# One decoder kernel: the first weight block by halves, an operand in one run, bias copies in the first MLP, dilated attention by head pairs, the last tile by halves

## Chip, cores and metric

One Trainium2 chip, one core. The metric is the time of one execution in device microseconds (us), all three transformer parts in one launch. Engines are named as in the profile: PE (TensorE), DVE (VectorE), ACT (ScalarE), POOL (GpSimd), SP (SyncE, which issues every DMA); PEld is PE's weight load.

## What is computed

256 tokens of width 1024 in float32 pass a gated-linear-attention layer with an MLP, a sliding-window-attention layer with an MLP, and a second block with two attentions, two gates, an MLP and a gated extra input:

```python
h = h + gla_mixer(rmsnorm(h), a_w_in, ...)          # 4 heads, chunks of 64
h = h + (relu(rmsnorm(h) @ w_up) ** 2) @ w_down     # MLP 1, 1024 -> 4096 -> 1024
h = h + swa_mixer(rmsnorm(h), ...)                  # 16 heads of 64, window 128, bias by distance
h = h + MLP 2
x = rmsnorm(h, ln_final)
z = rmsnorm(x) @ w_in_2                              # qa ka va | qb kb vb | ga gb
y_a = full attention, 8 heads of 128, axial rope     # "full"
y_b = for 4 head indices h, over 3 dilations g:      # "dilated", 12 heads of 64
      sc = q k^T + bias[g, h];  softmax over all 3 x 256 keys together;  sum p v
x = x + (sigmoid(ga + b) * (y_a @ w_a) + sigmoid(gb + b) * (y_b @ w_b)) @ w_out_2
x = x + MLP 3
x = x + sigmoid(rmsnorm(x) @ w_ple_gate) * (p @ w_ple)
out = rmsnorm(x)
```

## The kernel before

Every large product runs as three products of rounded parts (`prod`, L272): stationary high by moving high, high by low, low by high. A weight block of 2048 columns of 128 partitions (1 MB) passes through rings of three: SP loads it into `raw`, ACT rounds it into `whi` (`highs_to`), DVE subtracts for `wlo` (`lows_to`, two halves). SP issues block j when `wlo` of block j-3 is there. 160-odd blocks follow one another in the order of the products; `weights_to(n)` in `sync_program` (L2295) places the other loads between them by block number. Blocks 0 to 12 are the first layer's input (0, 1: q; 2: a narrow gate; 3, 4: k; 5 to 8: v; 9 to 12: gate), 13 to 16 its output, 17 to 48 MLP 1. All DMAs are issued by SP into one queue.

The activations are transposed on PE (`norm_turn`), evicted by ACT as high part and by DVE as low part into `hT`. In the up projection (`gemm_up`, L318) the weights are stationary and one product takes high and low of `hT` together through `hT2` (512 columns, two runs of 256 that lie 2048 elements apart), a second the high part alone with the low weights (256 columns). The down projection has the activations stationary and 512 weight columns moving.

Every engine runs generators that are interleaved by hand: `run_all((a, 1), (b, 2))` takes one step of a and two of b in turn until both end. In the dilated attention (PE L764, DVE L1464, ACT L2025) the work is by head index h (4) and half of the queries c (2): PE computes the scores of three dilations (64 rows of the array, 3 products), DVE adds the bias and takes the maximum, ACT the exponential with its sum, DVE the shares, PE six transposes, ACT copies them out of PSUM, PE six products with the values (64 columns of the array). It is interleaved with the weight products of gate `ga` (8 steps of 12 products), then the full attention (`full`, L852) with those of gate `gb` (8 steps). Each attention's last heads run after the last step.

The bias by distance is built once: rows of table values go to DRAM (`scr1`, `scr2`), and two DRAM-to-DRAM copies spread them to `toe1` (16 x 128 x 256) and `toe2` (12 x 128 x 384), each row shifted by one. They stand before `weights_to(9)` (L2331 to L2334), and the tables are read into SBUF later (`bias`, L2340 and L2342).

The window attention (`swa`, PE) already works on two heads at a time, in rows 0 to 63 and 64 to 127 of the array for the scores and in columns 0 to 63 and 64 to 127 for the values, one head's products after the other's in the order of the program.

At the end `w_ple_gate` is multiplied in two column halves f and two token halves c; ACT takes the sigmoid, DVE multiplies and adds to x, ACT squares with a sum, POOL makes the root, DVE scales x, SP writes four tiles.

## Time and profile before

| | us |
|---|---|
| median of 3 runs (lowest, highest) | 1064.34 (1063.89, 1066.04) |
| the profiled execution | 1064.24 |
| its span | 1062.4 |
| PE busy | 1012.1 |
| DVE busy | 676.2 |
| ACT busy | 489.3 |
| PE's share of the chain that ended last | 85% |

The span is from the first to the last instruction. A PE product is counted with its drain, so neighbouring products overlap in the records, and a busy PE can still be waiting between them; the distance between starts tells the pace. PEclk is the granted clock as a share of 2.4 GHz. The chain of waits follows the last instruction back, at each step to what released it.

### The profile page before, as it was taken

The page shows a single profiled execution, that of the slowest core. Times are in us where ns is not written, and L with a number is a line of the kernel's source. Part 1 is how long each engine was busy: PE and PEld are TensorE (multiplying, and loading weights), DVE is VectorE, ACT ScalarE, POOL GpSimd, SP SyncE. Part 2 cuts the span into 40 slices and gives each one's busy share as a digit, 9 for nine tenths or more (in the row PEclk, how much of TensorE's full clock was granted, in tenths as well). Part 3 has the DMA queues.
Part 4 walks back from the last instruction along what each step waited for, and adds up shares of the span by engine and source line. Part 5 has one row for each costly group of instructions (what it writes and reads, how often), then busy time and mean ns, then how long its engine had stood idle before and what let it go on. Part 6 is the DMA issues. An engine that isn't in the chain of part 4 may idle for free.

```text
span 1062.4 us, 12980 instructions
## 1 busy us (share of the span) xinstructions
PE 1012.1 (95%) x5384; PEld 849.5 (80%) x5384; DVE 676.2 (64%) x945; ACT 489.3 (46%) x573; POOL 42.8 (4%) x57
## 2 busy tenths in 40 slices
PE   6989999999999889999999999899999999999996
PEld 5866778888888767888888889877877788888875
DVE  4665766566656885754666656676656675466664
ACT  4353445344445653544444454334563454344452
POOL 1000100000000000000000013300000000000000
PEclk9989999999999999999999999999999999999999
DMA  7772376545564314765455555632335656545451
GB/s 214 249 262 80 119 238 224 173 160 197 199 214 143 120 50 149 250 217 197 159 188 180 201 183 161 196 100 80 99 109 178 195 175 215 188 159 197 180 175 43
DMA packets 115027, 180.99 MB, mean 170 GB/s; under 512 B 4351, under 2 KB 78567, under 8 KB 114968
## 3 DMA queue, kind: packets, MB, share of 16 engines
q1 hardware_dynamic: 114968, 180.16, 50.8%
q8 instruction: 42, 0.69, 0.3%
q14 instruction: 17, 0.14, 0.0%
HBM read 179.05 MB, written 5.55 MB: 174 GB/s over the span
## 4 chain that ended last, share of the span: by engine, by line
PE 85%; DVE 7%; ACT 2%; DMA 2%; POOL 2%; issue 1%; SPq 0%; DVEq 0%; POOLq 0%; ACTq 0%
PE ps L265 82%; PE ps L269 3%; DMA raw<-in_a_w_in 2%; DVE wlo L941 2%; DVE M L949 1%; DVE M L941 1%; POOL st L2186 1%; ACT M L1692 1%; ACT RR L1695 1%; ACT whi L1695 1%; POOL M L2186 0%; DVE M L945 0%; ACT M L1695 0%; DMA x<-in_x 0%; POOL st L2183 0%
## 5 line engine op out<-in xcount | busy, mean ns | idle before, releaser
L265 PE MATMUL ps<-whi,RR 128*128 128x512 f32 (+2 forms) x1568 | 494.6, 390 | 9.7 <-DVE wlo L941 6.0
L1695 ACT ACTIVATE whi<-raw 128x2048 fp32r<-128x2048 f32 (+1 forms) x161 | 302.3, 1881 | 196.6 <-PE ps L265 179.9
L941 DVE TENSOR_TENSOR wlo<-raw,whi 128x1024 fp32r<-128x1024 f32 (+1 forms) x322 | 372.5, 1200 | 29.9 <-ACT whi L1695 29.7
L265 PE MATMUL ps<-RR,whi 128*128 128x512 f32 (+1 forms) x1248 | 362.8, 357 | 10.9 <-DVE RR L949 5.6
L265 PEld LDWEIGHTS ps<-whi,RR 128*128 128x128 f32 x1568 | 293.9, 189 | 74.8 <-issue 9.6
L265 PE MATMUL ps<-wlo,RR 128*128 128x512 f32 (+2 forms) x784 | 303.2, 387 | 0.0
L265 PE MATMUL ps<-RR,wlo 128*128 128x256 f32 (+1 forms) x1008 | 284.5, 282 | 0.0
L265 PEld LDWEIGHTS ps<-RR,whi 128*128 128x128 f32 x1248 | 220.3, 190 | 50.6 <-issue 8.3
L265 PEld LDWEIGHTS ps<-RR,wlo 128*128 128x128 f32 (+1 forms) x1008 | 191.5, 190 | 0.9
L265 PEld LDWEIGHTS ps<-wlo,RR 128*128 128x128 f32 x784 | 148.4, 189 | 27.7
L941 DVE TENSOR_TENSOR M<-M,ps 128x512 f32<-128x512 f32 x56 | 38.5, 687 | 181.7 <-ACT M L1695 173.8
L1695 ACT ACTIVATE M<-ps 128x512 f32<-128x512 f32 (+2 forms) x97 | 57.1, 597 | 173.7 <-PE ps L265 138.5
L265 PE MATMUL ps<-M 128*64 128x128 f32 (+5 forms) x416 | 66.4, 334 | 5.6 <-DVE M L949 2.9
L265 PEld LDWEIGHTS ps<-M 128*64 128x64 f32 (+2 forms) x416 | 46.6, 163 | 22.1 <-issue 13.2
L1695 ACT ACTIVATE RR<-M 128x512 fp32r<-128x512 f32 x48 | 30.4, 633 | 71.1 <-DVE M L949 71.1
L2183 POOL TENSOR_SCALAR st<-st 128x2 f32<-128x2 f32 (+3 forms) x13 | 7.7, 595 | 886.6 <-DVE st L1032 621.3
L269 PE MATMUL ps<-ident,M 128*128 128x128 f32 (+1 forms) x194 | 29.4, 290 | 13.3 <-DVE M L941 4.9
L1695 ACT ACTIVATE RR<-ps,G 128x256 fp32r<-128x256 f32 x64 | 25.1, 480 | 32.9 <-PE ps L269 32.8
L269 PEld LDWEIGHTS ps<-ident,M 128*128 128x128 f32 (+1 forms) x194 | 23.2, 148 | 20.9 <-issue 14.9
L949 DVE SCALAR_TENSOR_TENSOR M<-M 128x512 f32<-128x512 f32 (+1 forms) x49 | 34.4, 703 | 1.6
L949 DVE SCALAR_TENSOR_TENSOR RR<-ps,G,RR 128x256 fp32r<-128x256 f32 x64 | 26.4, 478 | 13.7 <-ACT RR L1695 13.7
L941 DVE TENSOR_TENSOR RR<-M,RR 128x512 fp32r<-128x512 f32 x48 | 32.9, 686 | 0.0
(88 smaller groups left out, 381.7 us busy)
## 6 DMA issues: line engine op xcount, KB each, us to landing
raw<-in_w_up SPq DMA_DIRECT2D x32, 1024.0 KB, 5.4
raw<-in_w_down SPq DMA_DIRECT2D x32, 1024.0 KB, 5.0
raw<-in_w_ff SPq DMA_DIRECT2D x32, 1024.0 KB, 5.3
raw<-in_w_in SPq DMA_DIRECT2D x23, 1024.0 KB, 5.1
raw<-in_a_w_in SPq DMA_DIRECT2D x12, 1024.0 KB, 7.1
raw<-in_a_w_out SPq DMA_DIRECT2D x4, 1024.0 KB, 5.0
raw<-in_b_w_q SPq DMA_DIRECT2D x4, 1024.0 KB, 5.3
raw<-in_b_w_out SPq DMA_DIRECT2D x4, 1024.0 KB, 5.0
```

What stands on the lines that cost most here:

```text
L265: return pe.matmul(out, lhsT, rhs, start=start, stop=stop, skip_group_check=True)
L269: return pe.transpose(out, in_, ident[0:n, 0:n])
L941: return dve.tensor_tensor(out, a, b, op)
L949: return dve.scalar_tensor_tensor(out=out, in0=a, scalar=s, in1=b, op0=op0, op1=op1)
L1692: return act.activation(out, in_, f, **k)
L1695: return act.activation(out, in_, ACT.Copy, **k)
L2183: return pool.tensor_scalar(out, a, s1, s2, op0, op1)
L2186: return pool.tensor_tensor(out, a, b, op)
```

## The change

- `hT` and `hT2` share one layout, high and low of a chunk side by side: the 512 columns are one run.
- Block 0 is loaded, rounded and subtracted by halves, ahead of the second half of x, and its products begin with the first four chunks. Nine products of ones (`spin`) stand before the transposes. PE's row scale and the first eviction move behind block 1.
- `toe1` and `toe2` are written in four copies each, behind blocks 19 to 26; the first `bias` load moves from block 21 to 30.
- Dilated attention by pairs of head indices p (2) and halves c: six score products alternate between the rows of the array, twelve value products between its columns; one reduction, two exponentials and two shares. ACT copies the 768 columns in one instruction; its order is in the diff. PSUM banks 3, 4, 5 hold the scores, 6 and 7 the transposes, 2 the outputs. It runs beside ten steps of the gates' products, the full attention beside the remaining six.
- The last column half is cut in tiles `LAST` of 512, 256 and 256; the gain is multiplied in while the root is made, DVE and ACT each scale one token half.

The diff, cut to its core:

```diff
-        self.hT, self.yT = parts(0), parts(4096)
-        self.hT2 = RR[:, 0:4096].rearrange("p (a k t) -> p k a t", a=2, t=T)
+        self.hT2 = RR[:, 0:4096].rearrange("p (k n) -> p k n", k=8)
+        self.hT, self.yT = (self.hT2[:, :, 0:T], self.hT2[:, :, T:2 * T]), parts(4096)
...
-ORDER_D = [(h, c) for h in range(4) for c in range(2)]
+ORDER_D = [(p, c) for p in range(2) for c in range(2)]
+LAST = [(0, 0, 512), (1, 0, 512), (0, 512, 1024), (1, 512, 768), (1, 768, 1024)]
...
-                        for w_ in due(ready(k)):
+                        for w_ in due(K.at("w_lo", (0, 0) if j == 0 and k < 4 else j), ready(k)):
                             pe.wait_ge(*w_)
...
+                        mm(b[:, i, :], hi[:, k, 128 * i:128 * i + 128], V.hT2[:, k, :], k == 0, False)
                         t = mm(b[:, i, T:2 * T], lo[:, k, 128 * i:128 * i + 128], hT[0][:, k, :], False, k == 7)
...
+    def spin(n):
+        for w in due(K.at("ones")):
+            pe.wait_ge(*w)
+        for _ in range(n):
...
     def after_qk(f):
-        if f == 0:
+        if f == 256:
             rows_scale(0)
         count["qk"] += 1
-    g = gemm_a(("qk",), W, 0, 1024, hT, h_ready(0), None, after_qk)
+    g = gemm_a(("qk",), W, 0, 1024, hT, h_ready(0), lambda: None, after_qk)
     for _ in range(4):
         next(g)
...
+            tile = ("ds", p, c)
+            take(tile, 3, 4, 5)
...
-                t = mm(out, V.QB[r0:r0 + 64, hh // 2, c * 128:c * 128 + 128], V.KB[r0:r0 + 64, hh // 2, :], True, True)
+            for j, g in ((0, 2), (0, 0), (1, 1), (0, 1), (1, 2), (1, 0)):
+                if (j, g) == (1, 0):
+                    for w in due(K.at("ds_mid", (p, c))):
+                        pe.wait_ge(*w)
+                r = slice(64 * j, 64 * j + 64)
+                t = mm(b[:, 768 * j + 256 * g:768 * j + 256 * g + 256], V.QB[r, 2 * g + p, c * 128:c * 128 + 128],
+                       V.KB[r, 2 * g + p, :], True, True)
+                if (j, g) == (0, 2):
+                    t.then_inc(*K.up("ds_mid", (p, c)))
...
+            tile = ("dt", p, c, j)
+            take(tile, 6, 7)
...
+                take(tile, 2)
             b = K.bank(tile)
...
+                K.value["di_read", (p, c)] = K.full(tile)
             else:
-                t.then_inc(*K.up("di_read", (h, c)))
+                t.then_inc(*K.up("di_read", (p, c)))
         scores(*ORDER_D[0])
-        for i in range(11):
-            if 0 <= i - 1 < 8:
...
+        for i in range(4):
+            if i:
+                values(*ORDER_D[i - 1])
+            turned(*ORDER_D[i], 0)
+            yield
+            turned(*ORDER_D[i], 1)
+            if i < 2:
+                scores(*ORDER_D[i + 2])
+            yield
+        values(*ORDER_D[3])
     def rope():
...
-    gg = gemm_b(("ga",), W2, 3840, 1024, hT, ready, pairs=0)
+    def gates_b():
+        yield from gemm_b(("ga",), W2, 3840, 1024, hT, ready, (0, 0))
+        yield from gemm_b(("gb",), W2, 4864, 1024, hT, ready, (0, 1))
+    gg = gates_b()
     mix = dilated()
     next(mix)
-    run_all((gg, 1), (mix, 2))
-    gg = gemm_b(("gb",), W2, 4864, 1024, hT, ready)
+    for _ in range(10):
+        next(gg)
+        next(mix, None)
...
+    ready = h_ready(6)
+    for f in (0, 512):
+        bs = acc_pair()
+        tiles = [(("pg", i), take(("pg", i), misc() if i == 4 else bs[LAST[i][0]])) + LAST[i]
+                 for i in range(5) if LAST[i][1] // 512 * 512 == f]
+        for k0 in (0, 4):
+            j, hi, lo = block(A["w_ple_gate_2"][0][k0 * 128:k0 * 128 + 512, f:f + 512], 4, 512)
+            for tile, b, c, n0, n1 in tiles:
...
+                    t = prod(b[:, 0:n1 - n0], hT[0][:, k, c * 128:c * 128 + 128], hT[1][:, k, c * 128:c * 128 + 128],
+                             hi[:, k - k0, n0 - f:n1 - f], lo[:, k - k0, n0 - f:n1 - f], k == 0, k == 7)
...
-    norm_rest(0)
-    lows_to(1)
+    def first_low(i):
+        h = slice(1024 * i, 1024 * i + 1024)
+        for w in due(K.at("w_hi", (0, 0) if i == 0 else 0)):
+            dve.wait_ge(*w)
+        tt(V.lo[:, 0, h], V.raw[:, 0, h], V.hi[:, 0, h].bitcast(F32), ALU.subtract).then_inc(
+            *K.up("w_lo", (0, 0) if i == 0 else 0))
+    norm_early(0)
+    first_low(0)
+    norm_turn(0, 2)
+    norm_turn(0, 3)
+    first_low(1)
+    block["lo"] = 1
     squares(0, *all_x(K, 0))
...
-                V.BB[:, h:h + 5:4, c0:c0 + 256], ALU.mult, ALU.add)
-            stt(s[:, 512:768], b[:, 1, 0:256], rs, V.BB[:, 8 + h, c0:c0 + 256], ALU.mult, ALU.add).then_inc(
+            for w in due(K.full(tile), K.dma("bias", 1), *rb(4), *([K.full(("dt", p - 1, c, 1))] if p else [])):
+                dve.wait_ge(*w)
+            b = K.run(tile, 1536)
+            for j in range(2):
+                h = slice(768 * j, 768 * j + 768)
+                t = stt(s[:, h].rearrange("p (g k) -> p g k", g=3), b[:, h].rearrange("p (g k) -> p g k", g=3),
+                        st[:, 6 + c:7 + c], V.BB[:, 2 * p + j:2 * p + j + 9:4, c0:c0 + 256], ALU.mult, ALU.add)
+            t.then_inc(*K.emptied(tile))
+            for w in due(K.empty(tile)):
+                dve.wait_ge(*w)
+            dve.tensor_reduce(v[:, 0:2], s.rearrange("p (j k) -> p j k", j=2), AX, ALU.max, negate=True).then_inc(
+                *K.up("di_max", (p, c)))
+        def shares(p, c):
+            v = cc(p, c)
+            for j in range(2):
+                s = V.di_s(c)[:, 768 * j:768 * j + 768]
+                for w in due(K.at("di_exp", (p, c, j))):
+                    dve.wait_ge(*w)
+                d = step(dve.reciprocal(v[:, 4 + j:5 + j], v[:, 2 + j:3 + j]))
+                for w in due(d):
+                    dve.wait_ge(*w)
+                ts(s, s, v[:, 4 + j:5 + j], None, ALU.mult, None).then_inc(*K.up("di_p", (p, c, j)))
+        def parts(p):
+            tile = ("do", p)
+            for w in due(K.at("di_hi", p)):
+                dve.wait_ge(*w)
...
+        d = step(tt(s, s, V.PW[:, c, n0:n1], ALU.mult))
+        for w in due(d, K.full(("nt", 6, 3)), x_ready(K, 6, c, n)):
+            dve.wait_ge(*w)
+        tt(xc, xc, s, ALU.add).then_inc(*K.up("x_end", i))
+    def gain(i):
...
+    take()
+    gain(0)
+    gain(1)
+    take()
+    for i in (2, 3, 4):
+        add(i)
+    for i in (2, 3, 4):
+        gain(i)
+    for n in range(2):
+        s = V.SG[:, 1, 512 * n:512 * n + 512]
+        for w in due(K.at("rstd", ("end", 1)), K.at("x_gain", 4)):
+            dve.wait_ge(*w)
+        ts(s, s, st[:, 49:50], None, ALU.mult, None).then_inc(*K.up("y_end", (1, n)))
...
-    norm_rest(0)
-    highs_to(1)
+    def first_high(i):
+        h = slice(1024 * i, 1024 * i + 1024)
+        for w in due(K.dma("w_first") if i == 0 else K.dma("w0", 0)):
+            act.wait_ge(*w)
+        copy(V.hi[:, 0, h], V.raw[:, 0, h]).then_inc(*K.up("w_hi", (0, 0) if i == 0 else 0))
+    norm_early(0)
+    first_high(0)
+    norm_turn(0, 2)
+    norm_turn(0, 3)
+    first_high(1)
+    block["hi"] = 1
     squares(0, *all_x(K, 0))
...
+        soft(*ORDER_D[0])
+        yield
+        yield
+        soft(*ORDER_D[1])
+        yield
+        for i in range(4):
+            turned(i, 0)
+            if 0 < i < 3:
+                soft(*ORDER_D[i + 1])
+            if i == 2:
+                parts(0)
+            yield
+            turned(i, 1)
+            if i < 3:
+                yield
+        parts(1)
...
+    def square(i):
+        c, n0, n1 = LAST[i]
+        for w in due(K.at("x_end", i)):
+            act.wait_ge(*w)
+        actf(V.PW[:, c, n0:n1], x[:, c, n0:n1], ACT.Square, scale=1.0 / 32, accum_out=st[:, 40 + i:41 + i]).then_inc(
+            *K.up("end_sq", i))
...
+        for w in due(K.at("rstd", ("end", 0)), K.at("x_gain", 2)):
+            act.wait_ge(*w)
+        copy(s, s, scale=st[:, 48:49]).then_inc(*K.up("y_first", (0, n)))
...
     xd = A["x"].rearrange("a (c p) d -> p (a c) d", p=128)
     for n in range(2):
         load("x%d" % n, 0, V.x[:, :, n * 512:n * 512 + 512], xd[:, :, n * 512:n * 512 + 512])
+        w = K.blocks[0][0][512 * n:512 * n + 512, :] if K.blocks else A["a_w_in"][0][0:512, 0:256]
+        load("w0" if n else "w_first", 0, V.raw[:, 0, 1024 * n:1024 * n + 1024].rearrange("p (k n) -> p k n", k=4),
+             w.rearrange("(k p) n -> p k n", p=128))
+    state["block"] = 1
     weights_to(4)
     n = 0
...
     weights_to(9)
     for n in range(2):
...
+    for i in range(4):
+        weights_to(19 + i)
+        load("toe1", i, A["toe1"][4 * i:4 * i + 4], bass.AP(tensor=A["scr1"].tensor, offset=127 + 383 * 4 * i, ap=[
+            [383, 4], [-1, 128], [1, 256]]), K.dma("scr1"))
+    for i in range(4):
+        weights_to(23 + i)
+        load("toe2", i, A["toe2"][3 * i:3 * i + 3], bass.AP(tensor=A["scr2"].tensor, offset=127 + 511 * 3 * i, ap=[
+            [511, 3], [-1, 128], [1, 384]]), K.dma("scr2", 2))
+    weights_to(30)
+    load("bias", 0, V.BS, A["toe1"].rearrange("h p c -> p h c"), K.dma("toe1", 3), K.full(("to", 1, 1)))
     weights_to(62)
-    load("bias", 1, V.BB, A["toe2"].rearrange("h p c -> p h c"), K.dma("toe2"), K.empty(("pr", 1, 1)))
+    load("bias", 1, V.BB, A["toe2"].rearrange("h p c -> p h c"), K.dma("toe2", 3), K.empty(("pr", 1, 1)))
     load("lnf", 0, M[:, 0:1024], spread(A["ln_final"]))
     weights_to(109)
...
-    load("bg", 1, V.BG2, spread(A["b_gate_2"][:, 1024:2048]), K.full(("do", 1)))
+    load("bg", 1, V.BG2, spread(A["b_gate_2"][:, 1024:2048]), K.full(("dt", 1, 1, 1)))
     weights_to(117)
     load("p", 0, V.PT, A["p_2"][0, 0].rearrange("(c p) n -> p c n", p=128), K.full(("fv", 7)))
...
-                 V.x[:, c, n * 512:n * 512 + 512], K.at("y_end", (c, n)))
+                 V.SG[:, c, n * 512:n * 512 + 512], K.at("y_end" if c else "y_first", (c, n)))
     for name, n in K.n.items():
         if name.startswith("d_"):
```

## Rows read from the trace of the kernel before

**Rows 1.** Busy time by stretch: stretch, length, engines' busy us, PEclk, DMA share, GB/s
```profile
58.00:66.00 8.00, 3.76 (x17) 2.83 (x16) 3.69 (x4) 4.66 (x4) 0.20 (x1) 0.91 0.80 288
66.00:71.40 5.40, 5.40 (x14) 4.14 (x14) 4.34 (x4) 5.40 (x6) 0.00 (x0) 0.50 0.61 201
130.00:333.00 203.00, 200.76 (x1024) 170.06 (x1022) 125.76 (x143) 93.86 (x86) 1.09 (x3) 1.00 0.59 197
141.00:150.00 9.00, 9.00 (x50) 7.67 (x49) 5.17 (x8) 5.30 (x6) 0.00 (x0) 1.00 1.09 356
```

**Rows 2.** The chain of waits to 80 us: start, us, what
```profile
14.38 17.45 PE ps L265 x122
...
40.08 21.20 DMA raw<-in_a_w_in
...
65.67 8.42 PE ps L265 x24
74.08 0.44 PE ps L269 x4
```

**Rows 3.** Timeline of SP, PE and DVE at the hole: start, us, engine, line, operation
```profile
37.69 2.34 SPq L2293 DMA_DIRECT2D toe<-scr  x2
...
61.04 0.39 PE L265 MATMUL ps<-whi,RR 128*128 128x512 f32 x1
...
55.55 2.43 DVE L1222 TENSOR_TENSOR_SCAN M<-scan,M 128x256 f32<-128x256 f32 x4
```

**Rows 4.** Timeline of ACT at the start
```profile
6.65 3.40 ACT L1695 ACTIVATE RR<-ps,G 128x256 fp32r<-128x256 f32 x8 [1.74 <-PE ps L269]
9.94 1.91 ACT L1695 ACTIVATE whi<-raw 128x2048 fp32r<-128x2048 f32 x1
```

**Rows 5.** Timeline of PE, layer 1 and MLP 1; last row: chain of waits
```profile
23.79 0.28 PE L265 MATMUL ps<-RR,wlo 128*128 128x256 f32 x1
...
24.15 0.28 PE L265 MATMUL ps<-RR,wlo 128*128 128x256 f32 x1
...
205.31 0.39 PE L265 MATMUL ps<-RR,whi 128*128 128x512 f32 x1
205.54 0.28 PE L265 MATMUL ps<-RR,wlo 128*128 128x256 f32 x1
...
216.60 0.40 PE L265 MATMUL ps<-whi,RR 128*128 128x512 f32 x1
216.84 0.40 PE L265 MATMUL ps<-wlo,RR 128*128 128x512 f32 x1
...
1026.68 4.09 PE ps L265 x18
```

**Rows 6.** Timeline of PE in the window attention: scores, then values of a pair
```profile
364.17 0.93 PE L265 MATMUL ps<-M 64*128 64x128 f32 x8
...
365.84 1.14 PE L265 MATMUL ps<-M 128*64 128x128 f32 x12
```

**Rows 7.** Timeline of PE in the dilated attention: a round's parts
```profile
712.30 0.47 PE L265 MATMUL ps<-whi,RR 128*128 128x512 f32 x1
...
715.24 3.01 PE L265 MATMUL ps<-M 64*128 64x256 f32 x18
```

**Rows 8.** Timeline of PE in the full attention: its last rounds and the next projection
```profile
774.29 1.03 PE L265 MATMUL ps<-M 128*128 128x256 f32 x4
...
784.73 0.60 PE L269 MATMUL ps<-ident,M 128*128 128x128 f32 x4
...
788.23 0.47 PE L265 MATMUL ps<-whi,RR 128*128 128x512 f32 x1 [1.02 <-DVE RR L941]
```

**Rows 9.** Timeline of DVE in the dilated attention: the maximum of one head
```profile
706.16 0.95 DVE L1482 TENSOR_REDUCE cc<-M 128x1 f32<-128x768 f32 x1
```

**Rows 10.** Timeline of the end: the last sigmoid and the last scaling
```profile
1053.89 0.67 ACT L1692 ACTIVATE M<-ps,st 128x512 f32<-128x512 f32 x1
...
1058.34 1.41 DVE L949 SCALAR_TENSOR_TENSOR x<-x,st,M 128x512 f32<-128x512 f32 x2 [1.00 <-POOL st L2186]
```

More of the change, by code:

```diff
@@ L91, in pair, with run @@
         return self.banks[:, b:b + 2, 0:n]
+    def run(self, tile, n):
+        b = self.tile[tile][0] if tile in self.tile else 0
+        m = (n + 511) // 512
+        return self.banks[:, b:b + m, :].rearrange("p b n -> p (b n)")[:, 0:n]
     def vacant(self, tile):
@@ L492, in mlp @@
         last_chunk(7)
+    def spin(n):
+        for w in due(K.at("ones")):
+            pe.wait_ge(*w)
+        for _ in range(n):
+            mm(K.banks[:, 3, 0:128], V.S["ones"][:, :], V.S["ones"][:, :], True, True)
+    spin(4)
     tile = ("g", 0)
@@ L764, in dilated, with scores @@
     def dilated():
[L765 to L768 removed]
+        def scores(p, c):
+            tile = ("ds", p, c)
+            take(tile, 3, 4, 5)
+            b = K.run(tile, 1536)
             for w in due(K.empty(("qb", 512)), K.empty(("kb", 512))):
                 pe.wait_ge(*w)
[L771 to L776 removed]
@@ L778, in turned @@
-        def turned(h, c):
-            tile = ("dt", h, c)
-            s = V.di_s(h, c)
-            take(tile, *misc_pair())
-            b = K.pair(tile, 512)
-            for w in due(K.at("di_p", (h, c))):
+            for j, g in ((0, 2), (0, 0), (1, 1), (0, 1), (1, 2), (1, 0)):
[7 more added lines that the diff above has]
+                    t.then_inc(*K.up("ds_mid", (p, c)))
@@ L784, in turned @@
+            t.then_inc(*K.filled(tile))
+        def turned(p, c, j):
+            tile = ("dt", p, c, j)
+            take(tile, 6, 7)
+            b = K.run(tile, 768)
+            for w in due(K.at("di_p", (p, c, j))):
                 pe.wait_ge(*w)
             for n in range(6):
-                out = b[:, 0, n * 128:n * 128 + 128] if n < 4 else b[:, 1, n * 128 - 512:n * 128 - 384]
-                t = tr(out, s[:, n * 128:n * 128 + 128])
+                t = tr(b[:, n * 128:n * 128 + 128], V.di_s(c)[:, 768 * j + n * 128:768 * j + n * 128 + 128])
@@ L788, in turned, with values @@
             t.then_inc(*K.filled(tile))
-        def values(h, c):
-            tile = ("do", h // 2)
-            p = V.di_p(c)
-            if (h % 2, c) == (0, 0):
-                take(tile, 2 + h // 2)
+        def values(p, c):
+            tile = ("do", p)
+            if c == 0:
+                take(tile, 2)
             b = K.bank(tile)
-            rows = slice(64 * (h % 2), 64 * (h % 2) + 64)
-            for w in due(K.empty(("dt", h, c)), *[K.empty(("vb", f, cc)) for f in (0, 512) for cc in range(2)]):
+            for w in due(*[K.empty(("dt", p, c, j)) for j in range(2)],
+                         *[K.empty(("vb", f, cc)) for f in (0, 512) for cc in range(2)]):
@@ L1566, in ev_gb @@
         tile = ("gb", f, c)
-        for w in due(K.full(tile), K.dma("bg", 1), K.full(("do", 1))):
+        for w in due(K.full(tile), K.dma("bg", 1), K.full(("dt", 1, 1, 1))):
             dve.wait_ge(*w)
@@ L1570, in ev_gb, with gates_b @@
             *K.emptied(tile))
-    gg = gemm_b(1024, 8, ev_ga)
+    def gates_b():
+        yield from gemm_b(1024, 8, ev_ga)
+        yield from gemm_b(1024, 8, ev_gb)
+    gg = gates_b()
     mix = dilated()
     next(mix)
-    run_all((gg, 1), (mix, 2))
-    gg = gemm_b(1024, 8, ev_gb)
+    for _ in range(10):
+        next(gg)
+        next(mix, None)
     oA = yT
@@ L2078, in scalar_program, with gates_b @@
     run_all((gb, 2), (rp, 1))
-    gg = gemm_b(1024, 8, lambda f, m, c: None)
+    def gates_b():
+        yield from gemm_b(1024, 8, lambda f, m, c: None)
+        yield from gemm_b(1024, 8, lambda f, m, c: None)
+    gg = gates_b()
     mix = dilated()
     next(mix)
-    run_all((gg, 1), (mix, 2))
-    gg = gemm_b(1024, 8, lambda f, m, c: None)
+    for _ in range(10):
+        next(gg)
+        next(mix, None)
     oA = yT
@@ L2169, in scalar_program, with sig @@
     run_all((g, 1))
-    run_all((gemm_b(1024, 8, ev_pg), 1))
+    def sig(i):
+        c, n0, n1 = LAST[i]
+        for w in due(K.full(("pg", i)), K.at("rstd", 6)):
+            act.wait_ge(*w)
+        actf(V.SG[:, c, n0:n1], K.bank(("pg", i))[:, 0:n1 - n0], ACT.Sigmoid, scale=st[:, 4 + c:5 + c]).then_inc(
+            *K.emptied(("pg", i)))
+    def square(i):
+        c, n0, n1 = LAST[i]
+        for w in due(K.at("x_end", i)):
+            act.wait_ge(*w)
+        actf(V.PW[:, c, n0:n1], x[:, c, n0:n1], ACT.Square, scale=1.0 / 32, accum_out=st[:, 40 + i:41 + i]).then_inc(
+            *K.up("end_sq", i))
+    take()
+    take()
+    for i in range(2):
+        sig(i)
+        square(i)
+    take()
+    take()
+    sig(2)
+    sig(3)
+    square(2)
+    sig(4)
+    square(3)
+    square(4)
+    for n in range(2):
+        s = V.SG[:, 0, 512 * n:512 * n + 512]
+        for w in due(K.at("rstd", ("end", 0)), K.at("x_gain", 2)):
+            act.wait_ge(*w)
+        copy(s, s, scale=st[:, 48:49]).then_inc(*K.up("y_first", (0, n)))
 def pool_program(pool, K, V):
```

205 lines of the change are left out of this document (80 added, 125 removed).

## The prediction

> **What bounds the kernel now.** The table of stretches comes first [rows 1]. TensorE (PE) is the bound almost everywhere: from 130 to 333 us, the first MLP, it is busy for 200.8 of 203 us, and the two later MLPs look the same. One place stands out: from 58 to 66 us it works 3.8 of 8 us, and from 66 to 71.4 us it is busy but its granted clock is 0.50, the lower level of 1.2 GHz. The chain of waits says why [rows 2]: 21.2 us of it are one transfer of weights into `raw`. The queue's own timeline [rows 3] shows what stands ahead of it, the two copies `toe<-scr` issued from 37.7 us on (4.25 MB, DRAM to DRAM). A second place is busy for another reason: the dilated attention, where PE works through small products one after the other [rows 7]. Last the start [rows 4] and the end [rows 10], where nothing overlaps.
>
> The profiled execution took 1064.24 us (span 1062.4), the median of the three runs is 1064.34; all sums are made against 1064.24.
>
> **Part 1, the first block by halves.** Now: eight evictions of the transposed x on ScalarE (ACT), 6.65 to 10.05, the 2048-column copy to `whi` (1.91), VectorE's (DVE) two subtractions, first product at 14.38 [rows 2, 4]. After: four evictions (3.40/8 = 0.425 each, 1.7) end at 8.35; half a copy, 1.05, ends at 9.4; half of the subtraction, 1.2, ends at 10.7; the product starts near 10.75. 14.38 - 10.75 = 3.6 us. The half's load goes ahead of x's second half, which comes about 1.4 us later for it (0.5 MB at the 356 GB/s of [rows 1]); PE waits for it in transposes that only the second half needs. Second half: four evictions and a half copy end at 12.2, DVE about 13.6. At the low clock the first half's 24 products take 24 x 0.21 = 5 us, to 15.9, so it is ready. The squares of x slip behind these; their reader, the row scale, is moved behind block 1. The nine `spin` products have 128 columns each and lie in PE's idle time before x arrives (5.5 us): free. Whether they bring the clock up earlier no row shows; x's transposes from 5.5 us on did not. Bounds: the clock may come up at the same moment as now, which takes half of the 3.6 away (1.8), or early enough to give 1.8 more (5.4). I take 3.6, with the low stretch behind the first product as long as it is.
>
> **Part 2, bias rows into the first MLP.** Without the two copies weight block 7 is no longer late. The last product before the hole starts at 61.04, the next could start at 61.27 and does at 65.67 [rows 2, 3]; the 24 products after it take 8.42 us where 24 x 0.227 = 5.45 is full clock's rate [rows 2, 5]. Gap 4.4 plus clock 3.0 is 7.4 us. What is late next: the transposes at 74.08 need DVE's `kd`. Its chain starts when the scan ends at 58.0 [rows 3]: a subtraction, three exponentials of 1.05 behind a table load of 1.28, three products of 1.2 with one block's subtractions (2.35) among them. Placed without the late block it ends at about 67.9 on today's clock of events, and PE would ask for it at 61.27 + 5.45 = 66.7. So 1.2 us are given back: 6.1 us, bounds 4 and 7.5.
> The copies now go one by one behind weight blocks 19 to 26. Their price there: from the issue of the first (37.7) to the landing of block 7 (61.3) are 23.6 us; less one block (1.05 MB / 356 GB/s = 2.95 [rows 1]) that leaves at most 20.6/8 = 2.6 us each. 2.95 + 2.6 = 5.55 us, and PE uses up a block in 24 products of 0.227 or 16 pairs of 0.353, 5.45 to 5.65 us [rows 5]. That is even, and three `raw` buffers lie between. Cost 0; if that cover is gone, see the last rival. The 2 MB load of `bias` moves from block 21 to 30, far ahead of its reader, the window attention.
>
> **Part 3, the operand in one run.** In each up projection the 512-column product reads `hT2` as two runs of 256; 3 MLPs x 256 = 768 such products. A pair (512 and 256 columns) takes (216.60 - 205.31)/32 = 0.353 us. Products of 512 alone take 4.09/18 = 0.227, of 256 alone (24.15 - 23.79)/3 = 0.120, together 0.347 [rows 5]. So 0.006 x 768 = 4.5 us look like a price of the two runs. But the first two-run product, which follows 512-column ones, takes only 0.23 (205.31 to 205.54), and a one-run 512 that follows a 256 takes 0.24 (216.60 to 216.84). The 6 ns go with the alternation of lengths, not with the runs, and the alternation stays. I take 0; bounds 0 and 6.
> The Trainium skill (TensorE: Matmul & The Clock Gate, Back-to-back issue gap) says that the spacing of a stream is set by the weight load and the matmul together, and its section LDWEIGHTS prices that load by columns alone. By it nothing would be gained here either.
>
> **Part 4, dilated attention by head pairs.** One round now is: six transposes 0.63, twelve weight products 2.94 (712.30 to 715.24), then scores and values of one head and half, 18 passes, 2.95 [rows 7]. These passes are 6 x 256 + 12 x 128 = 3072 columns in 3.01 us busy, 0.98 ns a column: one after the other. In the window attention the two heads of a pair lie in different halves of the array, and there 1536 columns of scores take 0.93 us, 0.61 ns a column, and 1536 of values 1.14 us, 0.74 a column [rows 6]: they run beside each other. The new code alternates the halves product by product (the window attention does one head after the other) and sends them to different banks. So I take the better one for both: 3072 x 0.60 = 1.85 us for the scores of a pair and half, 1.85 for its values. Four of each: 14.8 us, against 8 x 2.95 = 23.6.
> Now the order. Today the dilated stage runs with 8 steps of weight products from 693.2 to 746.3, and the full attention with 8, to the next projection's first product at 788.23 [rows 8]: 95.0 us. After, 10 and 6. Dilated: 10 x 2.94 + 14.8 + 8 x 0.63 = 49.2. Full: six rounds as now, 746.3 to 774.3 (28.0). Behind them two heads are left with no weight products beside them: their values, transposes and scores, then reduction, exponentials and shares of the last head, one behind the other (2.8 us for a head), then from the last transposes to the projection 788.23 - 784.73 = 3.5 [rows 8]. Laid out, that is 9.8 us, where today 13.9 pass (774.29 to 788.23). 49.2 + 28.0 + 9.8 = 87.0; 95.0 - 87.0 = 8.0 us. Of the two moved steps (5.9 us) a third is lost at the end of the full attention.
> Does DVE keep up? For one pair and half: bias additions 2 x 1.0, maximum over 1536 about 1.75 (0.95 for 768 [rows 9]), the wait for the first exponential 1.1, two shares 1.5, 1.25 weight blocks at 2.35 = 2.9, a gate eviction 0.75: 10.0 us. PE's time for one is 49.2/4 = 12.3. Laying the two orders side by side I find no place where PE waits. ACT has 2 x 1.15 + 2 x 0.8 + 1.25 x 1.9 = 6.3. PE's wait on its own first score (`ds_mid`) has four products between and is free; only one score queues behind it. On SP, the load of `BG2` waits for the last dilated transposes instead of the last values; behind it stand only weight blocks of the next projection, due some 45 us later. Bounds: 0.98 ns a column after all leaves -1; 0.5 in both gives 10.5.
>
> **Part 5, the last tile by halves.** Two tiles of 256 columns instead of one of 512 add 24 x (0.240 - 0.227) = 0.3 us of PE. Behind it now: sigmoid 0.67, two DVE steps 1.4, square and its read, three POOL steps, two DVE steps 1.41 from 1058.34 [rows 10]: the last output is issued 5.9 us after PE. After: sigmoid, product, sum and square at half width (0.45, 0.42, 0.42, 0.6), a POOL step less (0.3), the gain already multiplied in, and last DVE steps of 0.45: 4.2 us. 5.9 - 4.2 - 0.3 = 1.4, bounds 0.5 and 2.
>
> **Sum.** 3.6 + 6.1 + 0 + 8.0 + 1.4 = 19.1; 1064.2 - 19.1 = 1045.1 us. The clock can move this by some 2 us either way, if other waits of PE bring it down than today's.
>
> **Rivals.** (a) The two runs do cost PE: part 3 brings 4.5 to 6, 1045.1 - 4.5 = 1040.6 or somewhat less. For it speaks 0.353 against 0.347; against it the two rows at the ends of the stretch. Chance 0.23.
> (b) DVE becomes the bound of the pairs, or the halves of the array don't run beside each other: part 4 brings 2 instead of 8.0, 1051.1 us. For it: DVE's 10.0 of 12.3 us; against it: the overlap of [rows 6]. Chance 0.16. The Trainium skill (TensorEngine Tiling (Array Packing), Performance Considerations) warns of this: tiling speeds up the products but not their eviction, which may become the bottleneck.
> (c) Slower than before: the copies starve the first MLP, behind blocks 19 to 27. If each copy's 2.6 us falls on PE whole, that is 21 us, and if a third of the holes bring the clock down as the one at 61 us did (3.0 each), 8 more: 1045.1 + 29 = 1074. It decides from where a copy takes over 2.7 us, and only after the spare of two buffers (11 us) is used up. Against it: 2.6 is an upper bound, beside other loads. Chance 0.04.
> The forecast keeps 0.57.
>
> **Numbers.** Predicted 1045.1 (its own range 1041 to 1049.5). The range reaches to (a) with a good start and to (b): 1036.5 to 1052.5; outside lie (c) and the far ends. About 0.2% (2 us) can be told from no change: faster 0.95, same 0.01, slower 0.04.
>
> **What would show it.** First product at 10.5 to 11 us. No PE hole at 58 to 66, full clock there, `kd` just in time. In the up projections still 0.353 for a pair; 0.347 would be rival (a). The dilated stage from first scores to first full scores 49 us, scores plus values of a pair and half near 3.7; 5.9 would be (b). Around blocks 19 to 27 (155 to 190 us) PE dense; holes there are (c). Output issued 4.2 us after the last product. What would make it wrong above all: a chain of DVE and ACT in the first layer that was hidden behind the hole at 61 us.

## The result, and the profile after

The changed kernel takes 1074.48 us (median, 1072.57 to 1075.74) where the kernel before took 1065.19 in the same comparison: ratio 1.0087, 95% interval 1.0064 to 1.0109. It is slower, by 9.3 us; forecast was 1045.1. Its profiled execution has a span of 1074.0 us.

Where the time went is read from stretches between the same large waits of PE in both traces. First two such stretches of the kernel before: the first MLP, and dilated plus full attention (stretch, length, busy us of the engines, PEclk, DMA share, GB/s).

```profile
150.55:331.89 181.34, 179.94 (x923) 152.67 (x921) 112.47 (x126) 83.38 (x75) 1.09 (x3) 1.00 0.56 188
686.74:786.82 100.08, 96.27 (x502) 77.78 (x501) 66.58 (x119) 44.61 (x90) 0.84 (x1) 0.98 0.32 105
```

The same view of the kernel after, first the stretch that answers to the hole of [rows 1], then both of these, and four short ones.

```profile
60.00:66.00 6.00, 5.84 (x25) 4.56 (x26) 6.00 (x7) 4.28 (x4) 0.00 (x0) 1.00 0.60 182
142.61:344.82 202.21, 186.53 (x923) 157.06 (x921) 112.45 (x126) 83.24 (x75) 1.09 (x3) 0.96 0.58 195
700.07:798.73 98.66, 88.07 (x502) 70.92 (x501) 64.31 (x107) 44.01 (x82) 0.82 (x1) 0.95 0.33 106
142.00:144.00 2.00, 0.88 (x9) 0.64 (x6) 0.84 (x3) 1.52 (x5) 0.00 (x0) 1.00 0.27 88
180.00:185.00 5.00, 5.00 (x21) 4.29 (x20) 0.00 (x0) 0.90 (x1) 0.00 (x0) 0.61 0.20 74
719.80:724.80 5.00, 0.34 (x2) 0.00 (x0) 4.85 (x8) 4.42 (x6) 0.00 (x0) 0.84 0.20 32
724.80:730.00 5.20, 5.13 (x20) 3.88 (x21) 0.00 (x0) 0.83 (x2) 0.00 (x0) 0.50 0.44 171
```

- The hole at 61 us is gone and the clock is full there. The first MLP begins 7.9 us earlier (150.55 to 142.61).
- The first MLP takes 202.2 us instead of 181.3, 20.9 more: PE stands still for 14.3 us more (15.7 against 1.4) and is busy for 6.6 more (186.5 against 179.9), at a granted clock of 0.96 instead of 1.00. That is the whole loss, and more.
- Dilated and full attention together take 98.7 instead of 100.1: 1.4 us gained where 8.0 were forecast. PE has 8.2 us less to do, but now waits 10.6 us instead of 3.8, and at 720 us it stands still for nearly 5 us, with the lower clock behind it.
- From the last large gap (1030.39 before, 1042.66 after) to the end of the span it is 32.0 before and 31.3 after.

PE's four holes in it, in its own timeline (the first two rows are up projections, the others down projections):

```profile
177.97 0.77 PE L275 MATMUL ps<-RR,whi 128*128 128x512 f32 x1 [2.99 <-DVE wlo L987]
188.55 0.47 PE L275 MATMUL ps<-RR,whi 128*128 128x512 f32 x1 [2.07 <-DVE wlo L987]
200.58 0.80 PE L275 MATMUL ps<-whi,RR 128*128 128x512 f32 x1 [6.24 <-DVE wlo L987]
211.05 0.69 PE L275 MATMUL ps<-whi,RR 128*128 128x512 f32 x1 [2.98 <-DVE wlo L987]
```

The chain of waits of the kernel after in the first MLP (start, us, what):

```profile
151.80 10.98 DMA raw<-in_w_down
...
166.83 17.24 DMA raw<-in_w_up
184.07 0.02 issue
184.10 1.90 ACT whi L1786
186.00 18.86 DMA raw<-in_w_down
```

47 us of the chain are weight loads. ACT's timeline shows their rhythm: it rounds each block when it has landed.

```profile
162.81 1.92 ACT L1786 ACTIVATE whi<-raw 128x2048 fp32r<-128x2048 f32 x1 [1.54 <-DMA raw<-in_w_down]
173.52 1.92 ACT L1786 ACTIVATE whi<-raw 128x2048 fp32r<-128x2048 f32 x1 [6.20 <-DMA raw<-in_w_up]
184.10 1.92 ACT L1786 ACTIVATE whi<-raw 128x2048 fp32r<-128x2048 f32 x1 [8.66 <-DMA raw<-in_w_up]
194.42 1.91 ACT L1786 ACTIVATE whi<-raw 128x2048 fp32r<-128x2048 f32 x1 [8.41 <-DMA raw<-in_w_down]
```

A block arrives every 10.3 to 10.7 us, while PE uses one up in 5.45 to 5.65 [rows 5]. Between two blocks stands one bias copy of 3 heads, and while it runs the DMA engines are busy for 0.20 (180 to 185 us above), about 3 of 16; a copy of 4 heads runs at 0.27 (142 to 144), about 4 of 16. 3 heads of 128 x 384 numbers are 0.59 MB, at 74 GB/s 8.0 us; with 2.95 for the block behind it [rows 1] that is an estimate of 10.9, close to the rhythm seen. So the theory: a copy is spread over as many DMA engines as it has heads in its outermost dimension, and the next block, which needs all 16, waits for these few. The Trainium skill states the rule (DMA: Bandwidth & Descriptors, section on why a DMA increments its semaphore by 16): the number of engines is the largest up to 16 that divides the outermost size of both sides. The two shares agree with it. The prediction did not draw on this page.

### The profile page after: what moved, and what is told of

Its sections match the earlier page's. It is cut to its first block, busy times and chain, and to the rows that moved or that the text cites. A ratio compares the mean times of both kernels' runs of the same rounds, so it can differ in the third digit from the quotient of the medians.

```text
span 1074.0 us, 13061 instructions
## 1 busy us (share of the span) xinstructions
PE 1014.1 (94%) x5426; PEld 850.0 (79%) x5426; DVE 674.1 (63%) x938; ACT 490.1 (46%) x571; POOL 44.3 (4%) x58
## 3 DMA queue, kind: packets, MB, share of 16 engines
HBM read 179.05 MB, written 5.55 MB: 172 GB/s over the span
## 4 chain that ended last, share of the span: by engine, by line
PE 77%; DVE 10%; DMA 4%; ACT 3%; issue 2%; POOL 2%; POOLq 0%; DVEq 0%; ACTq 0%
PE ps L275 74%; DVE wlo L987 3%; DMA raw<-in_w_down 3%; PE ps L279 3%; DVE M L995 2%; DMA raw<-in_w_up 2%; DVE M L987 1%; ACT whi L1786 1%; ACT M L1783 1%; POOL st L2322 1%; DVE M L991 1%; ACT M L1786 1%; ACT RR L1786 0%; POOL M L2322 0%; DVE RR L995 0%
## 5 line engine op out<-in xcount | busy, mean ns | idle before, releaser
L275 PE MATMUL ps<-whi,RR 128*128 128x512 f32 (+2 forms) x1584 | 496.7, 389 | 15.1 <-DVE wlo L987 12.3
L1786 ACT ACTIVATE whi<-raw 128x2048 fp32r<-128x2048 f32 (+2 forms) x162 | 302.5, 1871 | 222.7 <-PE ps L275 177.3
L275 PE MATMUL ps<-RR,whi 128*128 128x512 f32 (+1 forms) x1248 | 365.6, 359 | 12.3 <-DVE wlo L987 6.5
L275 PEld LDWEIGHTS ps<-RR,whi 128*128 128x128 f32 x1248 | 221.2, 191 | 53.7 <-issue 10.3
L1786 ACT ACTIVATE M<-ps 128x512 f32<-128x512 f32 (+1 forms) x89 | 56.5, 635 | 150.9 <-PE ps L275 133.1
L275 PE MATMUL ps<-M 128*64 128x128 f32 (+5 forms) x416 | 56.3, 342 | 6.5 <-DVE M L995 2.9
L275 PEld LDWEIGHTS ps<-M 128*64 128x64 f32 (+2 forms) x416 | 38.6, 166 | 20.2 <-issue 11.7
L2319 POOL TENSOR_SCALAR st<-st 128x2 f32<-128x2 f32 (+2 forms) x11 | 7.6, 692 | 905.1 <-DVE st L1078 640.9
L995 DVE SCALAR_TENSOR_TENSOR M<-ps,st,M 128x512 f32<-128x512 f32 (+2 forms) x32 | 22.8, 746 | 16.8 <-PE ps L275 16.8
```

Source lines behind the costliest of these rows:

```text
L275: return pe.matmul(out, lhsT, rhs, start=start, stop=stop, skip_group_check=True)
L995: return dve.scalar_tensor_tensor(out=out, in0=a, scalar=s, in1=b, op0=op0, op1=op1)
L1786: return act.activation(out, in_, ACT.Copy, **k)
L2319: return pool.tensor_scalar(out, a, s1, s2, op0, op1)
```

## Experiments

All times are medians beside runs of the kernel before on the same chip; the ratio has its 95% interval.

**Copies by rows, all else as after.** Each piece takes 32 of the 128 rows of every head, so that the outermost dimension is 16 or 12 heads. The edit, with its names shortened:

```
-load("toe1", i, A["toe1"][4*i:4*i+4], AP(scr1, 127 + 383*4*i, [[383, 4], [-1, 128], [1, 256]]))
+load("toe1", i, A["toe1"][:, 32*i:32*i+32], AP(scr1, 127 - 32*i, [[383, 16], [-1, 32], [1, 256]]))
-load("toe2", i, A["toe2"][3*i:3*i+3], AP(scr2, 127 + 511*3*i, [[511, 3], [-1, 128], [1, 384]]))
+load("toe2", i, A["toe2"][:, 32*i:32*i+32], AP(scr2, 127 - 32*i, [[511, 12], [-1, 32], [1, 384]]))
```

> The kernel after, with the eight bias copies cut by rows (32 rows of all 16, or all 12, heads) instead of by heads (all 128 rows of 4, or 3, heads); same bytes, same places behind blocks 19 to 26. Theory S (spread): a copy of 4 or 3 heads goes over only 4 or 3 of the 16 DMA engines (in the trace of after their share is 0.25 and 0.20 while one runs alone), and each weight block behind needs these engines too. Cut by rows a copy takes 16 or 12 engines and 1.6 to 2.5 us: the first MLP loses its 20.9 us, time 1074.5 - 20.9 = 1053.6 (1052 to 1057). Rival B (bytes): what costs is the 4.25 MB between DRAM and DRAM at a time when the weights have no spare; then the cut changes nothing, 1072 to 1076. Half way, 1060 to 1066, would mean both.

Measured 1053.12 us, ratio 0.9897 (0.9882 to 0.9912). The same bytes at the same places cost nothing any more: the first MLP, and ACT's rhythm in it, in the trace of this kernel:

```profile
141.15:322.51 181.36, 179.96 (x922) 152.66 (x921) 112.46 (x126) 83.50 (x75) 1.10 (x3) 1.00 0.62 213
```

```profile
154.30 1.90 ACT L1786 ACTIVATE whi<-raw 128x2048 fp32r<-128x2048 f32 x1
159.96 1.90 ACT L1786 ACTIVATE whi<-raw 128x2048 fp32r<-128x2048 f32 x1
165.61 1.90 ACT L1786 ACTIVATE whi<-raw 128x2048 fp32r<-128x2048 f32 x1
```

181.36 us against 181.34 before, and 5.65 us a block, without a wait for a load. Rival B falls. SP's rows show one thing more, here the issue of a weight load behind the last copy in the kernel after, then one with copies by rows:

```profile
186.00 9.22 SPq L2442 DMA_DIRECT2D raw<-in_w_down  x1
```

```profile
167.34 0.37 SPq L2442 DMA_DIRECT2D raw<-in_w_down  x1
```

Behind each of the four copies of 3 heads the load of a block keeps SP at its issue for 5.6 to 9.2 us; the four loads of the same stretch with copies by rows keep it for 0.4 each. Whether a block is late because the few engines are taken, or because SP is held up at issuing it, no run separates. Both go with the narrow copies.

**Copies at their old place, all else as after.** The loops of four are taken out, the two whole copies stand ahead of weight block 7 again, and the first `bias` load behind block 21.

> The kernel after, with the two bias copies whole and back at their old place, ahead of weight block 7; the load of the first biases back behind block 21. Undoes part 2 alone. If part 2 is all that went wrong in the first MLP: minus 20.9 there, plus some 6.6 in the first layer (the transposes of the decayed keys near 72.5 instead of 65.9), 1074.5 - 14.3 = 1060.2. If the first MLP's loss came from another part (the operand in one run), its end stays 14 us late and the time is 1074.5 + 6.6 = 1081.

Measured 1059.54, ratio 0.9958 (0.9939 to 0.9977). The first MLP is 181.34 us again: the loss is part 2's alone.

**Part 2 alone, as written, on the kernel before.**

> The kernel before with part 2 alone as it is written (copies of 4 and 3 heads in the first MLP). Theory S: 1065.2 - 6.5 + 20.9 = 1079.6 (1077 to 1082). If the parts hang together (the earlier start is what starves the first MLP) it is nearer to 1065.2 - 6.5 = 1058.7.

Measured 1078.54, ratio 1.0138 (1.0123 to 1.0153); first MLP 202.3 us. The earlier start has no share in it.

**Part 2 alone, copies by rows.**

> The kernel before with part 2 alone, but the copies cut by rows. Theory S: the first layer gains 6.5 and the first MLP pays at most 1: 1058.7 (1057.5 to 1060). Rival B (bytes): as with copies by heads, near 1079.6.

Measured 1059.03, ratio 0.9953 (0.9939 to 0.9968). The transposes of `kd`, at 74.08 before [rows 2], come at 67.70, and the first MLP is 181.3 us.

```profile
67.70 0.63 PE L269 MATMUL ps<-ident,M 128*128 128x128 f32 x4
```

**Part 2 alone, the first four copies by rows, the last four by heads.**

> The kernel before with part 2 alone, the first four copies by rows (16 DMA engines) and the last four by heads (3 engines). Sum of theory S, per block behind a copy by heads: the engines that the copy holds need 2.95 us for the block and 7.9 for the copy of 3 heads (5.6 for one of 4), PE uses a block up in 5.65. So a copy of 3 heads throws the loads 5.2 us back, one of 4 heads 2.9; all eight 32.4, of which the buffers take some 11 and 21 remain (20.9 measured in the first MLP). Here 4 x 5.2 = 20.8, less 11: the first MLP pays 10, and the time is 1059.0 + 10 = 1069 (1066 to 1072). If each copy by heads cost the same (20.9/8 = 2.6), it is 1069.5 too, and the holes tell: none ahead of the third of the last four copies by theory S. If a few small copies are free as such, it is 1059.

Measured 1073.65, ratio 1.009 (1.0073 to 1.0107). First MLP 196.5 us: 15.2 more than before, outside the expected range. ACT's timeline shows the same rhythm as above, blocks at

```profile
168.69 1.92 ACT L1695 ACTIVATE whi<-raw 128x2048 fp32r<-128x2048 f32 x1 [0.56 <-DMA raw<-in_w_up]
179.22 1.92 ACT L1695 ACTIVATE whi<-raw 128x2048 fp32r<-128x2048 f32 x1 [8.61 <-DMA raw<-in_w_up]
189.85 1.91 ACT L1695 ACTIVATE whi<-raw 128x2048 fp32r<-128x2048 f32 x1 [8.72 <-DMA raw<-in_w_down]
200.53 1.92 ACT L1695 ACTIVATE whi<-raw 128x2048 fp32r<-128x2048 f32 x1 [6.17 <-DMA raw<-in_w_down]
```

every 10.5 to 10.7 us. PE stands still for 1.73 + 6.45 + 2.58 = 10.8 us in the three holes, close to the sum of 10; the other 4.4 us are PE's work at the lower clock behind holes, which the sum had left out. The first hole waits for the block behind the second of these copies, one copy earlier than expected. For all eight copies the sum gave 21 of standing still alone; the trace of part 2 alone has 1.77 + 4.69 + 5.12 + 3.08 = 14.7, plus 6.2 from the clock. So the sum holds for copies of 3 heads and is too dear for those of 4, which cost 5.7 us all four together (20.9 - 15.2).

**Part 2 alone, copies by heads as written, but one behind every third block.**

In short:

```
-weights_to(19 + i) ... weights_to(23 + i) ... weights_to(30)
+weights_to(19 + 3 * i) ... weights_to(31 + 3 * i) ... weights_to(42)
```

> The kernel before with part 2 alone, the copies by heads exactly as written (4 and 3 heads), but one behind every third weight block (19, 22, ... 40) instead of every block, and the load of the first biases behind block 42. Theory S as a rate: a copy throws the loads back 2.9 or 5.2 us, and the two blocks between give 2 x 2.7 = 5.4 back, so that the spare of the buffers is never used up: the first MLP pays at most 1 and the time is 1059.0 (1058 to 1061). If a copy over few engines costs PE 2.6 us each wherever it stands, it is 1079.

Measured 1058.64, ratio 0.9948 (0.9928 to 0.9968), first MLP 181.35 us. The slow copies themselves cost PE nothing; what cost was one after every block, so that the spare time of the loads never caught up.

**ScalarE's first turned copy ahead of the second exponentials** (with copies by rows, all parts).

```
         soft(*ORDER_D[0])
         yield
         yield
+        turned(0, 0)
         soft(*ORDER_D[1])
         yield
         for i in range(4):
-            turned(i, 0)
+            if i:
+                turned(i, 0)
```

In the trace of the kernel after, PE's second transposes wait 4.74 us, and ACT's timeline shows for what:

```profile
724.87 1.54 PE L279 MATMUL ps<-ident,M 128*128 128x128 f32 x6 [4.74 <-ACT M L1786]
```

```profile
714.87 1.90 ACT L1786 ACTIVATE whi<-raw 128x2048 fp32r<-128x2048 f32 x1
720.38 0.94 ACT L1783 ACTIVATE M<-M,cc 128x768 f32<-128x768 f32 x1 [3.61 <-DVE cc L1543]
...
722.23 1.90 ACT L1786 ACTIVATE whi<-raw 128x2048 fp32r<-128x2048 f32 x1
724.03 0.79 ACT L1786 ACTIVATE M<-ps 128x768 f32<-128x768 f32 x1
```

The last row is the copy that frees the transposes' banks. Its input is there at about 717.4, while ACT is idle; but it is queued behind two exponentials that wait for DVE's maximum (till 720.34) and behind a rounding of weights.

> The kernel after with copies by rows (1053.1 us), and one edit on ScalarE in the dilated attention: the copy of the first turned probabilities goes ahead of the second pair's exponentials instead of behind them. Theory O (order): the hole of 4.84 us at 697 us in the trace of the kernel with copies by rows, and the low clock of some 7 us behind it (2.5 us of PE), come from TensorE's second transposes waiting for that copy, which stands on ScalarE behind exponentials that wait for VectorE's second maximum. Then 7.3 us are gained: 1053.1 - 7.3 = 1045.8 (1044.5 to 1047). Rival V (VectorE is the bound of the pairs): the hole moves to the next thing that waits for VectorE, 1051 to 1053.

Measured 1046.97, ratio 0.9836 (0.9814 to 0.9858), the fastest kernel of this study. The stretch, ACT, and PE in its trace:

```profile
679.94:770.13 90.19, 83.79 (x503) 67.59 (x501) 63.99 (x107) 44.01 (x82) 0.82 (x1) 1.00 0.35 116
```

```profile
696.18 0.81 ACT L1786 ACTIVATE M<-ps 128x768 f32<-128x768 f32 x1 [0.65 <-PE ps L279]
699.13 0.94 ACT L1783 ACTIVATE M<-M,cc 128x768 f32<-128x768 f32 x1 [2.14 <-DVE cc L1543]
```

```profile
698.74 0.82 PE L279 MATMUL ps<-ident,M 128*128 128x128 f32 x6
699.49 1.67 PE L275 MATMUL ps<-M 64*128 64x256 f32 x12
704.02 1.53 PE L275 MATMUL ps<-M 128*64 128x128 f32 x24
```

DVE's maximum comes no earlier against PE's work than before the edit (2.14 us of ACT's wait are still its own), but no PE instruction waits behind it. Rival V falls. The stretch takes 90.2 instead of 98.7 us, 8.5 less: 4.7 of standing still, 2.5 of the lower clock behind it, and the rest mostly a spell of lower clock over 20 transposes at 703 us, which took 4.04 us in the kernel after and here 2.37. That last part is not the edit's: the transposes stand ahead of it, they took 4.02 us in the kernel before too, and only this trace and that of the pairs with the edit (below) are without the spell. The same kernel without the spin products (last run on part 1, below) has it again, 4.04 us, and this stretch:

```profile
679.56:770.93 91.37, 85.45 (x502) 69.25 (x501) 64.30 (x107) 44.02 (x82) 0.84 (x1) 0.98 0.34 114
```

That is 7.3 us less than with copies by rows and the old order (98.6), as theory O said; by the medians it is 6.2 (1053.12 to 1046.97). The scores and values of a pair and half take 1.67 and 1.53 us.

**The pairs alone, on the kernel before, without and with that edit.**

> The kernel before with the dilated attention by head pairs alone. From the two traces (the stretch from the norm before it to the end of the full attention is 100.1 us before and 98.65 after): 1064.1 - 1.4 = 1062.7 (1061.5 to 1064).

Measured 1063.52, ratio 0.9987 (0.9973 to 1.0001), so the times alone don't tell it from no change; stretch 98.4 us.

> The kernel before with the dilated attention by head pairs and ScalarE's first copy of turned probabilities ahead of the second exponentials. Theory O: 1062.7 - 7.3 = 1055.4, that is the 8.0 us and a little more that the sum gave to part 4. Rival V: 1061 to 1063.

Measured 1055.09, ratio 0.9909 (0.9886 to 0.9931); stretch 90.2 us, with the 20 transposes at full clock (2.37 us). By the medians the edit is worth 8.4 us here.

**Part 1 alone, with and without the nine spin products.**

> The kernel before with part 1 alone (first block by halves, spin, qk scale moved). The kernel with the bias copies at their old place reached the norm ahead of the first MLP 4.6 us earlier than before, and its other parts don't touch that stretch: 1064.1 - 4.6 = 1059.5 (1058.5 to 1061). If the 3.6 us were eaten by the late block 7, which comes on DMA's time and not on PE's, it is 1063 to 1064.

Measured 1061.62, ratio 0.9975 (0.9961 to 0.9988): 2.9 us less by the medians, outside the expected range and between its two cases. The 4.6 us came from one trace. There the hole ahead of block 7 was 2.20 us, with full clock behind it; in the trace of part 1 alone it is 4.52, and from 58 to 66 us the granted clock is 0.72. In four traces whose first layer keeps its order (the kernel before and parts 3, 4 and 5 alone) this hole was 4.24, 4.04, 2.94 and 3.67 us, and the first MLP began up to 1.4 us apart. So a difference of 1 to 2 us in the first layer is not settled by one pair of traces.

> The kernel before with part 1 alone but without the nine small spin products (with them: 1061.6, full clock from 10 us on in the trace). Prediction's view: spin is free and does nothing, the time is the same, 1061 to 1062. Rival C (clock): spin is what lets the first block run at the full clock; without it the first 24 to 48 products run at the lower level (8.55 us for 48 instead of 6.0), as before the change. Even then the end moves little, since the next products wait for weight blocks that come on DMA's time: 1061.6 to 1064.

Measured 1062.37, ratio 0.9970 (0.9953 to 0.9987).

> The fastest kernel so far (all parts, bias copies by rows, ScalarE's first turned copy ahead: 1047.0) without the nine spin products. If spin is without effect 1046 to 1048. If it holds the clock up in the first layer 1048 to 1050.

Measured 1047.13, ratio 0.9828 (0.981 to 0.9845), against 1046.97 with spin. The spin products do nothing that can be measured, and the prediction's view of them holds. Part 1 without them, 1062.37, lies in rival C's range and 0.4 us outside the other, too close to tell by the time; the traces decide. Rival C wanted some 8.5 us for the first 48 products, as before the change. Without spin they take 6.8 us here and 7.2 in the kernel with all parts; with it they take 6.0 in three traces and 7.4 to 7.5 in two, that of part 1 alone among them, whose granted clock from 8 to 16 us was 0.79, not the full clock that the expectation gives it. What lies just ahead of them is PE's own work on x, not 5.2 us of idleness as before the change; that this is the reason was not tried. The clock falls later too, and not in each execution. PE in the trace with all parts and the edit, 30 to 36 us, and in that of part 1 without spin, 32 to 36 us:

```profile
30.00:36.00 6.00, 6.00 (x25) 4.92 (x24) 3.84 (x5) 3.03 (x2) 0.00 (x0) 0.50 0.63 200
```

```profile
32.00:36.00 4.00, 4.00 (x30) 3.47 (x29) 3.11 (x4) 0.91 (x1) 0.00 (x0) 1.00 0.47 174
```

All traces with part 1 have the same wait of PE of 0.29 us at 29 us, for an eviction that DVE reaches late; the kernel before has none there. In six of the seven the clock is at the lower level behind it for a time (the next 24 products take 5.48 us in the kernel after and 4.64 in that of part 1 alone), in one, part 1 without spin, it isn't (3.13). What decides was not tried.

**Part 5 alone.**

> The kernel before with part 5 alone (last tile by halves, gain ahead). In the traces the last step on VectorE ends 1.4 us earlier against the last large gap, as predicted, but the four stores of 256 KB are then issued within 2.0 us instead of 3.4, and the last bytes land 0.7 us later behind it: 1064.1 - 0.7 = 1063.4 (1062.8 to 1064).

Measured 1064.32, ratio 1.0005 (0.9994 to 1.0017): no difference, and the 0.7 us that were expected are not seen. The trace of the kernel after shows both sides of it, first ACT's last sigmoid and SP's stores, then the busy time of DMA to the end:

```profile
1066.55 0.47 ACT L1783 ACTIVATE M<-ps,st 128x256 f32<-128x256 f32 x1
```

```profile
1069.39 1.97 SPq L2432 DMA_DIRECT2D out<-M  x4
```

```profile
1069.67 0.88 DVE L991 TENSOR_SCALAR M<-M,st 128x512 f32<-128x512 f32 x2 [0.46 <-POOL st L2322]
```

```profile
1070.00:1072.00 2.00, 0.00 (x0) 0.00 (x0) 0.56 (x2) 0.00 (x0) 0.00 (x0) 0.84 0.89 333
1072.00:1074.00 2.00, 0.00 (x0) 0.00 (x0) 0.00 (x0) 0.00 (x0) 0.00 (x0) 0.50 0.51 192
```

DVE's last step ends 4.0 us after the last sigmoid begins, 5.9 before [rows 10]. But the four stores now go out within 2 us instead of 3.4, and 1.05 MB have to leave at 333 GB/s: from DVE's end to the end of the span it is 3.4 us, 2.6 before.

**Part 3 alone.**

> The kernel before with part 3 alone, the operand of the up projections in one run of 512 columns. Theory of the prediction: 0 (within 0.7 us of before), a pair of products stays at 0.353 us. Rival (a): 1064.1 - 4.5 to 6 = 1058 to 1059.6.

Measured 1064.5, ratio 1.0 (0.9986 to 1.0013). PE in an up projection of this kernel:

```profile
205.41 0.40 PE L265 MATMUL ps<-RR,whi 128*128 128x512 f32 x1
205.64 0.28 PE L265 MATMUL ps<-RR,wlo 128*128 128x256 f32 x1
205.76 0.40 PE L265 MATMUL ps<-RR,whi 128*128 128x512 f32 x1
```

This block has 32 pairs. From the first at 205.07 to the product behind the last at 216.36 it is 11.29 us, 0.353 us for a pair as before [rows 5], though the 512 columns are one run; 0.347 would have been rival (a).

## Why the prediction was wrong, step by step

- **Part 1** (3.6 forecast): 2.9 alone, by the spans and by the medians, with about 1.4 us of doubt from the hole ahead of block 7. In the kernel after the first product starts at 11.46 instead of 10.75, since the transposes of x began at 6.32 instead of 5.50 in that execution; in the other traces with part 1 it is 10.4 to 10.6. The clock behind it was higher than forecast, that behind 30 us lower. Inside the bounds of 1.8 to 5.4.
- **Part 2, gain** (6.1): 6.2 us in the trace of part 2 by rows, up to the first MLP, with the same doubt. `kd`'s transposes follow at 67.70, where the reckoning of what is late next gave 66.7 + 1.2 = 67.9. Right.
- **Part 2, price** (0): 20.9 us. This is the step that made the sign wrong. The 2.6 us for a copy were taken as an eighth of the 23.6 us that both whole copies took. But the whole copies have 16 and 12 heads, and while they ran beside weight loads (41 to 56 us of the kernel before) the DMA share was 0.95; an eighth of them by heads runs at 0.27 or 0.20, some 4 or 3 engines: 0.52 MB at 88 GB/s are 6.0 us, 0.59 at 74 are 8.0. The balance of 5.55 against 5.45 to 5.65 us a block should have been 9 and 11, by these two figures and the 2.95. "An upper bound" was said of a number that was none: time per byte was carried from a transfer of one shape to one of another. The balance itself was the right test, and with copies by rows it holds to 0.02 us.
- **Rival (c)** was the right one, and its 1074 us the measured time: its mechanism, a rate of loads that PE outruns once the spare of the buffers is used up, is what the runs show; its 2.7 us and 11 us fit them, but were not measured by themselves. That it hit 1074 is partly luck: its 21 + 8 = 29 were 14.3 of standing still and 6.6 of lower clock, 20.9, and the difference is nearly made up by the 8.0 of part 4, of which 1.4 came. Its chance of 0.04 hung on the false bound.
- **Part 3** (0): 0. Right; the 6 ns go with the alternation of lengths. Rival (a) falls.
- **Part 4** (8.0): 1.4 us in the kernel after. The cost of the products was right and even too high: 1.67 + 1.53 = 3.2 us for a pair and half where 3.7 were forecast. The step that failed is "laying the two orders side by side I find no place where PE waits". It compared busy sums (DVE's 10.0 of 12.3 us) and missed ACT's order in the first round, where a copy that PE needs is queued behind an exponential that waits for DVE. That costs 4.7 us and 2.5 more of lower clock. With the copy ahead of it part 4 brings 9.5 us by the medians, and in the traces 9.9 where the 20 transposes ran at full clock and 8.7 where they ran at the lower level as before (91.4 against 100.1). The 8.0 and the 4 x 0.5 us by which the products were cheaper would be 10.0. Rival (b) named the right size (2 instead of 8.0) by a wrong cause: neither DVE nor the array is the bound.
- The Trainium skill's warning that was weighed there (TensorEngine Tiling (Array Packing), Performance Considerations) would have put the blame on eviction from the banks. The eviction in question takes 0.79 us, and moving it in ACT's queue was enough.
- **Part 5** (1.4): the chain is 1.9 us shorter, less 0.3 for PE; 0.8 is given back by the stores, which were half hidden before. 0.7 remains between the last large gap and the end in the kernel after, in one trace, and nothing measurable alone. The forecast counted to the issue of the last store, not to its landing.

The terms as measured: 1064.2 - 2.9 - 6.2 + 20.9 + 0 - 1.4 - 0.7 = 1073.9. With both orders mended, and part 4 at the same clock as before: 1064.2 - 2.9 - 6.2 - 8.7 - 0.7 = 1045.7 (1044.5 with 9.9); measured 1046.97. The 1 to 2.5 us between are not explained. This is in the range of the forecast, but it is another kernel: the forecast was made for the one with both faults.

## What to carry over

When a transfer is cut into pieces, look at what becomes of its outermost dimension before any time is carried over to the pieces: bytes are conserved, the number of DMA engines is not, and a small copy on few engines delays every full-width load queued behind it. Slow copies between loads are free only as long as the loads catch up between them, so compare the interval of the pieces with the interval in which a buffer is used up. And where work is paired or moved, follow each in-order queue through the first round, instruction by instruction: a sum of busy times does not show a cheap copy that stands behind a wait.
